# The gate and up biases of a mixture-of-experts kernel: two fp32r parts on 64 partitions instead of three bf16 parts on 96

## The reference, cut to what matters

```python
def clamped_swiglu(gu):
    gate = jnp.minimum(gu[..., :D_FF], SWIGLU_LIMIT)
    up = jnp.clip(gu[..., D_FF:], -SWIGLU_LIMIT, SWIGLU_LIMIT)
    return gate * jax.nn.sigmoid(SWIGLU_ALPHA * gate) * (up + 1.0)

def expert_block(args):            # 128 token slots of one expert
    xb, e = args
    gu = xb @ w_gate_up[e] + b_gate_up[e]      # (128, 1024) @ (1024, 2048) + (2048,)
    return clamped_swiglu(gu) @ w_down[e] + b_down[e]
```

## Time and profile before

| | us |
|---|---|
| median of 3 runs | 1812.04 (1810.42 to 1814.46) |
| the profiled execution | 1809.91 |
| its span | 1808.1 |
| granted TensorE clock, mean over the span | 0.945 |
| PE, DVE, ACT, POOL busy | 1674.7, 1363.2, 1097.6, 198.9 |

### The profile page before, as it was taken

The page is one execution under the profiler, slowest core; times in us unless marked ns, Lnnn a source line. Parts: engine busy times, 40 slices in busy tenths (PEclk is TensorE's granted clock), DMA queues, the critical chain, the costliest instruction groups (busy, mean ns, idle before and its releaser), DMA issues.

```text
span 1808.1 us, 19659 instructions
## 1 busy us (share of the span) xinstructions
PE 1674.7 (93%) x7500; PEld 1303.3 (72%) x7500; DVE 1363.2 (75%) x1009; ACT 1097.6 (61%) x901; POOL 198.9 (11%) x154
## 2 busy tenths in 40 slices
PE   6999997678578999999999999999999999999994
PEld 1688864444346888888888888888888888888872
DVE  0444447945456899989888988989898889989894
ACT  2322224441156777777777777777777777777771
POOL 2000000021200010010001001100100010011012
PEclk8899996688668999999999999999999999999997
DMA  7575522011479999999999999999999999999964
GB/s 238 168 273 199 199 98 66 1 50 70 140 265 379 366 357 383 387 384 365 383 383 361 379 385 380 368 394 385 366 374 384 384 363 392 382 372 361 383 230 152
DMA packets 157540, 540.15 MB, mean 299 GB/s; under 512 B 14988, under 2 KB 16120, under 8 KB 157330
## 3 DMA queue, kind: packets, MB, share of 16 engines
q1 hardware_dynamic: 140880, 500.20, 73.3%
q0 software_dynamic: 13424, 34.48, 7.9%
q10 hardware_dynamic: 3138, 4.21, 0.6%
HBM read 522.55 MB, written 29.26 MB: 305 GB/s over the span
## 4 chain that ended last, share of the span: by engine, by line
PE 74%; DVE 2%; ACT 1%; issue 1%; POOL 0%; POOLq 0%; ACTq 0%; DVEq 0%
PE ps L1067 64%; PE ps L638 3%; PE ps L1041 3%; PE ps L1057 2%; PE ps L701 1%; PE ps L658 1%; DVE wl L1182 0%; ACT wh L1115 0%; PE ps L651 0%; PE ps L440 0%; ACT h2t L727 0%; DVE y L796 0%; DVE yo L1325 0%; ACT junke L1350 0%; POOL rs L1735 0%
## 5 line engine op out<-in xcount | busy, mean ns | idle before, releaser
L1182 DVE TENSOR_TENSOR wl<-rawm,wh 128x2048 fp32r<-128x2048 f32 x420 | 946.5, 2288 | 174.6 <-ACT wh L1115 170.4
L1115 ACT ACTIVATE wh<-rawm 128x2048 fp32r<-128x2048 f32 x420 | 802.0, 1919 | 270.9 <-PE ps L1067 270.5
L1067 PE MATMUL ps<-wh,xh 128*128 128x512 f32 x1120 | 360.8, 403 | 18.5 <-DVE xl L1195 18.5
L1067 PE MATMUL ps<-wl,xh 128*128 128x512 f32 x1120 | 347.0, 391 | 0.0
L1067 PE MATMUL ps<-wh,xl 128*128 128x512 f32 x1120 | 346.8, 391 | 0.0
L1067 PEld LDWEIGHTS ps<-wh,xh 128*128 128x128 f32 x1120 | 211.8, 189 | 68.4 <-DVE xl L1195 19.9
L1067 PEld LDWEIGHTS ps<-wl,xh 128*128 128x128 f32 x1120 | 211.4, 189 | 45.0
L1067 PEld LDWEIGHTS ps<-wh,xl 128*128 128x128 f32 x1120 | 211.4, 189 | 44.6
L1067 PE MATMUL ps<-wh,ah 128*128 128x512 f32 x560 | 179.5, 402 | 7.6 <-DVE al L1199 7.6
L1067 PE MATMUL ps<-wl,ah 128*128 128x512 f32 x560 | 173.8, 392 | 0.0
L1067 PE MATMUL ps<-wh,al 128*128 128x512 f32 x560 | 173.0, 390 | 0.0
(11 more groups left out here) (243 smaller groups left out, 1610.4 us busy)
## 6 DMA issues: line engine op xcount, KB each, us to landing
rawm<-in_w_gate_up SPq DMA_DIRECT2D x280, 1024.0 KB, 9.6
rawm<-in_w_down SPq DMA_DIRECT2D x140, 1024.0 KB, 7.7
raw<-in_w_ada SPq DMA_DIRECT2D x24, 1024.0 KB, 5.2
raw<-in_w_in SPq DMA_DIRECT2D x16, 1024.0 KB, 5.3
wo<-in_w_out SPq DMA_DIRECT2D x2, 2048.0 KB, 16.4
bias_vectors_repeated<-bias_vectors POOLq DMA_DIRECT2D x1, 2304.0 KB, 15.6
xs<-in_x ACTq DMA_DIRECT2D x1, 2048.0 KB, 24.6
x1s<-in_x SPq DMA_DIRECT2D x4, 512.0 KB, 4.0
```

Source lines behind the costliest of these rows:

```text
L1067: ins = nc.tensor.matmul(banks[:, n, :], left[:, kk, :], right[:, k, n * UN:(n + 1) * UN], start=begins and kk == 0 and i == 0, stop=kk == ...
L1115: nc.scalar.activation(flat(wh[v % SPL][:]), flat(rawm[v][:]), ACT.Copy).then_inc(wh_done, 1)
L1182: nc.vector.tensor_tensor(flat(wl[v][:]), flat(rawm[v][:]), flat(wh[v % SPL][:]), ALU.subtract).then_inc(wl_done, 1)
```

## The change

Two parts instead of three, and fp32r instead of bf16. `ball`, `bparts` and `sel` shrink to 64 rows. VectorE still adds 1 to the up half (step 8). ScalarE then copies all of `ball` to `bparts` as fp32r (its step 9, the high part), and VectorE subtracts in rows 32 to 63 (its step 12, the low part). `bparts` now takes 8 KB a partition, so `bdn` moves to another address, for which GpSimd's load waits until the attention outputs are transposed, and SP's first gate loads until TensorE has used `bdn`. In the passes of the further blocks the column of `sel` is no longer addressed by a register of TensorE: ScalarE reads the expert's number, copies the column into `selc`, and TensorE waits for that.

```diff
-    ball = at("ball", [96, 2 * D], F32, 52 * KB)
+    ball = at("ball", [64, 2 * D], F32, 52 * KB)
-    bparts = at("bparts", [96, 2 * D], BF16, 180 * KB)
-    bdn = at("bdn", [E, D], F32, 184 * KB)
+    bparts = at("bparts", [64, 2 * D], F32R, 180 * KB)
+    bdn = at("bdn", [E, D], F32, 32 * KB)
-    sel = small("sel", [96, E + 1], BF16)
+    sel = small("sel", [64, E + 1], F32R)
+    selc = small("selc", [64, 1], F32R)
...
             if n == 0:
-                dve.wait_ge(ball_in, 16 * 3)
+                dve.wait_ge(ball_in, 16 * 2)
                 dve.wait_ge(latemod_ready, 3)
                 nc.vector.tensor_scalar(ball[:, D:2 * D], ball[:, D:2 * D], 1.0, None, ALU.add).then_inc(bias_step, 1)
-                dve.wait_ge(bias_step, 1)
-                nc.vector.tensor_copy(bparts[:], ball[:]).then_inc(bias_step, 1)
                 return
-            cut, lo = ((False, 1), (False, 2), (True, 1), (True, 2), (False, 2), (True, 2))[n - 1]
-            rows = slice(32 * lo, 32 * lo + 32)
-            dve.wait_ge(bias_step, n + 1)
-            if cut:
-                nc.vector.tensor_copy(bparts[rows, :], ball[rows, :]).then_inc(bias_step, 1)
-            else:
-                nc.vector.tensor_tensor(ball[rows, :], ball[rows, :], bparts[rows, :], ALU.subtract).then_inc(bias_step, 1)
+            dve.wait_ge(bias_step, 2)
+            nc.vector.tensor_tensor(bparts[32:64, :], ball[32:64, :], bparts[32:64, :], ALU.subtract).then_inc(bias_step, 1)
...
-            if 8 <= i < 8 + N_BIAS:
+            if i in (8, 12):
                 bias_parts(i - 8)
...
@@ attention_act, behind copies(i) and exps(i + AHEAD)
+            if i == 9:
+                act.wait_ge(bias_step, 1)
+                nc.scalar.activation(bparts[:], ball[:], ACT.Copy).then_inc(bias_step, 1)
...
@@ merge_pool
+        pool.wait_ge(ot_ps, TC)
         pool.dma_start(bdn[:], b_down[0]).then_inc(bdn_in, 16)
...
@@ experts_sync
         sp.wait_ge(xg_in, 16)
+        sp.wait_ge(init_ps, TC)
...
@@ experts_pe
-                nc.tensor.matmul(banks[:, n, :], sel[:, bass.ds(e, 1)].to_broadcast([96, P]),
+                nc.tensor.matmul(banks[:, n, :], (sel[:, e:e + 1] if isinstance(e, int) else selc[:]).to_broadcast([64, P]),
...
             if not is_first(p):
                 pe.wait_ge(u_ready, p)
+            if p >= E:
+                pe.wait_ge(selc_ready, p - E + 1)
             biased(UPPED, e, D)
...
@@ experts_act
+        def column_chosen(p):
+
+            if p == E:
+                act.wait_ge(plan_ready, 1)
+                act.sem_inc(passed, 1)
+            e = act.value_load(ptab[0:1, 0, p - E + 2:p - E + 3], min_val=0, max_val=E)
+            nc.scalar.activation(selc[:], sel[:, bass.ds(e, 1)], ACT.Copy).then_inc(selc_ready, 1)
...
                 acts_high(p)
                 outputs(p - 1, used(p, HALVES - 1), first=is_second(p))
+            if p >= E - 1:
+                column_chosen(p + 1)
             split_ahead(p, last)
...
-        for b in range(3):
+        for b in range(2):
             pool.dma_start(ball[32 * b:32 * b + 32, :], b_gate_up[0]).then_inc(ball_in, 16)
```

More of the change, by code:

```diff
@@ L73, in constants @@
     oh[:N_BUCKETS, 1], oh[N_BUCKETS, 1] = hot * causal, ~causal
-    sel = np.tile(np.eye(E, E + 1, dtype=np.float32), (3, 1))
+    sel = np.tile(np.eye(E, E + 1, dtype=np.float32), (2, 1))
     pick = np.concatenate([np.eye(E, E + 2, 1, dtype=np.float32), np.triu(np.ones((E, E + 2), np.float32), 2)], 1)
@@ L270, in program @@
     wsum = route("wsum", [P, 2, TC], F32)
-    self_ = route("self", [96, E + 1], F32)
+    self_ = route("self", [64, E + 1], F32)
     past = at("past", [1, MORE + 1, E], F32, 160 * KB)
@@ L333, in program @@
     N_W = N_T + N_N
-    N_BIAS = 7
     N_SMALL = 9
@@ L940, in program @@
     passed, tokens_in, scur_last = sem("passed"), sem("tokens_in"), sem("scur_last")
+    selc_ready = sem("selc_ready")
     N_GU, N_D = 8, 4
@@ L991, in further_blocks, with further_passes @@
         return eng.value_load(ntab[0:1, 0:1], min_val=0, max_val=MORE)
-    def further_passes(eng, count, body, j=0, d=E - 1):
+    def further_passes(eng, count, body, j=0, d=E - 1, e_of=planned_expert):
         if j == MORE:
@@ L997, in further_passes @@
         with eng.If(count >= j + 1):
-            e = planned_expert(eng, E + j)
+            e = e_of(eng, E + j)
             body(E + j, e, d)
-            further_passes(eng, count, body, j + 1, e)
+            further_passes(eng, count, body, j + 1, e, e_of)
     def experts_sync(sp):
@@ L1102, in experts_pe @@
         count = further_blocks(pe)
-        further_passes(pe, count, body)
+        further_passes(pe, count, body, e_of=lambda eng, p: None)
         pe.wait_ge(al_done, count + E)
```

## The result

The changed kernel takes 1840.21 us (median of 4 runs, 1837.38 to 1842.92), the kernel before 1813.1 in the same comparison (1810.42 to 1814.46): a ratio of 1.0159 [1.0145, 1.0172], 1.6% slower. The forecast was 1814.6 with a range of 1808 to 1820; the time lies 20 us above the range. The profiled execution took 1842.92, its span 1841.1, against 1808.1 before. The mean granted clock is 0.951 of 2.4 GHz, before it was 0.945, and from 600 to 1640 us it is 1.00 in both, so a lower clock is not what makes up most of the 33 us.

What follows compares the result with a forecast made beforehand. TensorE bounds the expert stage, VectorE the bias work in attention. Attention -6.9, bias matmuls 0, stalls +6.9, last column copy +0.2, clock falls +2.4 sum to +2.6 us; on the median 1812.0 that gave 1814.6, range 1808 to 1820.

Steps and rivals of the forecast that it cites:

- Part 2: Bias matmuls in the expert stage: same rate, longer weight loads hidden; 0 us, ends -0.5 and +12.6.
- the long weight loads show: Rival, bias matmuls: the extra 0.090 us of load is bare at each of 140; +12.6, 1827 us; chance 0.03.
- Part 1: Attention stage: fewer bias steps on VectorE, the bound engine there; gain 6.9 us, ends 4.5 and 9.6.
- Part 3: Three further passes: TensorE waits 2.3 us each for ScalarE's column, 6.9; clock falls 2.4, fourth copy 0.2 us.
- Part 4: GpSimd's down-bias load and SP's first gate loads shift later, covered by existing waits; no cost.
- Attention wins: Rival, attention stage: denser TensorE work holds 2.4 GHz longer; 1806.5 us, deciding from a gain of 10.7; chance 0.07.
- No stall: Rival, further passes: ScalarE has the column before TensorE ends its pass; -6.7, 1805.3 us; chance 0.03.

Runs made afterwards that it cites:

- doubled pair: The changed kernel with each bias pair followed by a second 64-row pair that multiplies by a column of zeros; 1870.52 us (one run).
- 96-row kernel: The changed kernel with its fp32r bias matmuls on 96 rows, the last 32 with a zero selector; 1816.12 us, ratio 1.0019 to the kernel before.

## Why the prediction was wrong

**The step that failed** is Part 2, the bias matmuls at nothing: "Same rate. The weight load gets longer [...] but 48 of those long loads pass behind their matmuls without a gap. So 0". Both halves of it hold by themselves. The rate is the same (0.22 each in the doubled pair), and loads of 0.189 do pass behind matmuls, on 128 rows and on 96. What I left unpriced was the number of rows itself: 96 became 64, I compared type and load length, and treated the rows as free. The term was 0 with an upper end of 12.6; it measured 28.4 in the 33 steady passes. The rival with the right sign, "the long weight loads show", had a chance of 0.03 and the wrong cause: the 96-row kernel keeps the long loads and loses nothing of that size. Its price was under half as well: it put 0.09 at each of 140 loads, where each of the 140 borders costs 0.20 (the pair, 0.65 against 0.45) or 0.22 (the block of expert matmuls behind it, 11.13 against 10.91, which I had counted as untouched).

The Trainium skill, "TensorEngine Tiling (Array Packing)", section "Key Properties", says that changing the tiling mode drains TensorE, and its section "Available Configurations" lists modes of 128, 64 and 32 rows and none of 96. I had looked for rules on the weight load and not on the shape. The trace agrees as to which rows pay: 0.20 to 0.23 us a border for 64 rows in fp32r, 0.15 for 64 and 32 rows in bf16, nothing for 96. The page gives no price. That the bias matmuls are such a change of mode is my reading; the runs show that the matmuls on the two sides of a border stand further apart, and not why.

The trace of before had a place that could have raised the question, and I read past it. The scores of the attention stage have 64 rows and stand among matmuls of 128:

```profile
301.82 0.30 PEld L397 LDWEIGHTS ps<-qk 64*128 64x128 f32 x4 [0.17 <-issue]
...
311.90 1.36 PEld L392 LDWEIGHTS ps<-ka,qk 64*128 64x128 f32 x8 [0.33 <-issue]
```

The loader waited for nothing in the profile and still stood. Had I put 0.17 (at 2.4 GHz) on four borders in each of 35 passes, the sum would have been 24 us. It would have been a guess, though: the same kind of idle, 0.26, stands ahead of the bf16 bias loads on 96 rows in that trace [0.26 at 1065.25, above] and costs nothing, and at 300.47 a load on 128 rows has 0.33. Such an idle time marks a place to test, and only the distance of the matmuls across it is a price.

**Part 1, attention: near in size, the agreement partly luck.** -6.9 forecast, -6.6 measured at the last transposition of one profile. Three other profiles of the same attention program, listed at the end, have 6.9 to 9.8, so that one is the smallest of the four. The wait for ScalarE's copy was 2.35 where I took 1.6 (1.3 to 1.9), because TensorE's wait grew from 2.65 to 5.31. The floor of 4.1 for two following units was too high: in the third block they came 3.4 apart. These two errors have opposite signs, and the clock, which the sum left out, was higher: 0.79 from 266 to 388 us against 0.70 before. How much each contributes was not separated. The remaining bias work is as forecast, one subtraction of 2.28 on VectorE and one copy of 1.89 on ScalarE.

**Part 3, the stalls: right.** Three of 2.29 (forecast 2.2 to 2.4), released by the selc line; the clock fell behind one of three, 1.6 (forecast 2.4 for one to two); the fourth copy is 0.19 of the chain (forecast 0.2). The 96-row kernel shows two falls of three; both lie in my "one to two".

**Part 4, free moves: no cost seen.** No wait in the chain of the expert stage belongs to them.

**The rivals.** "Attention wins" did not come in the changed kernel, but what it describes occurs: in two later profiles the stage ended 12.0 and 14.9 earlier, beyond the 10.7 that it asked for, at a mean clock of 0.85 and 0.89 instead of 0.70. "No stall" was refuted; made on purpose by the earlier column it was worth 8 us in the stage. With Part 2 at zero the forecast holds: the 96-row kernel's 1816.12 is 1.5 above it, inside the range.

## What to carry to other kernels

Before a matmul's contraction rows are cut, compare with its neighbours in the stream: 64 rows between matmuls of 128 cost 0.20 to 0.23 us at each border in fp32r, and 64 or 32 rows 0.15 in bf16, four times a pass here; padding to 96 with zeros took the price away, and putting the small matmuls side by side halved the number of borders. When an operand's shape changes, look in the trace for any instruction that already has the new shape beside the old one, and compare the distance of the matmuls across the border with their distance within a group; idle time of the loader alone can be free. A value that another engine makes for the next pass belongs where that engine is early, not at the end of its pass.

## What the hardware showed that I had not expected

- The price of a border depends on the type of the small matmul: 0.81 to 0.86 a pass in fp32r, 0.58 to 0.62 in bf16, though the expert matmuls beside it are the same.
- The idle ahead of a 64-row load in the attention stage of the kernel before is 0.17 where four matmuls of that line take 0.70 us (301.82), and 0.33 where the same four take 1.23 (290.62). The idle seems to follow the granted clock as the matmuls do; no run tested it.
- After the same idle of 2.29 us in the same stream the granted clock fell in one place and not in another. The 96-row kernel's chain, the block behind each of its three stalls (in the changed kernel it fell behind one of three):

```profile
1653.51 12.13 PE ps L1066 x48
...
1692.70 12.56 PE ps L1066 x48
...
1732.32 10.89 PE ps L1066 x48
```
- The attention stage's last transposition is at 380.38, 380.08, 377.53 and 377.18 in four kernels (the changed one, the earlier column, the pairs side by side, the second pair) whose program is the same up to there. A gain of 2 us in that stage can't be seen in a single run.
